# Two half-array matmuls for the second pass of the grouped-query scores

## The reference

```python
def attend(q, k, v):
    ...
    def block(qi):
        s = jnp.einsum('bkgqd,bksd->bkgqs', qi, k).astype(F32) * scale
        p = jax.nn.softmax(s, axis=-1).astype(v.dtype)
        return jnp.einsum('bkgqs,bkse->bkgqe', p, v)
...
gq_x = axial_rope(rms_norm(heads(x_gq, GQA_HEADS), gqa_q_norm_w[i]), ang_gqa)
gk_x = axial_rope(rms_norm(heads(x_gk, GQA_KV_HEADS), gqa_k_norm_w[i]), ang_gqa)
o_gqa = attend(gq_x, jnp.concatenate([gk_c, gk_x], axis=2), jnp.concatenate([gv_c, gv_x], axis=2))
```

## Time and profile before

| | |
|---|---|
| median of 3 runs | 3417.54 us (3416.53 to 3421.4) |
| the profiled execution | 3418.68 us |
| its span, first to last instruction | 3416.9 us |
| PE busy | 3356.0 us (98%) |
| DVE busy | 2267.3 us (66%) |
| ACT busy | 1252.6 us (37%) |
| POOL busy | 1012.0 us (30%) |
| mean granted TensorE clock | 0.997 |

### The profile page before, as it was taken

One profiled execution on the slowest core, in us unless ns is written; L12 is line 12 of the kernel. 1 busy time (PEld: TensorE's weight loads), 2 busy tenths in 40 slices (PEclk: granted clock), 3 DMA queues, 4 the chain that ended last, 5 costly groups with the idle time before them and its releaser, 6 DMA issues. The chain is left out here.

```text
span 3416.9 us, 49584 instructions
## 1 busy us (share of the span) xinstructions
PE 3356.0 (98%) x18300; PEld 2858.2 (84%) x18300; DVE 2267.3 (66%) x3536; ACT 1252.6 (37%) x2128; POOL 1012.0 (30%) x1121
## 2 busy tenths in 40 slices
PE   8999999999999999999999999999999999999998
PEld 4888888888888888888888788889998788888886
DVE  6574667887178888888855533478993656656566
ACT  4332356776142111111112532366773322222222
POOL 0232320111423333333334211410013343443433
PEclk9999999999999999999999999999999999999999
DMA  6455463121112222222110423562212111111111
GB/s 241 147 187 186 146 190 93 53 70 70 39 56 74 74 74 74 74 74 74 55 37 31 160 100 137 162 201 55 58 53 82 44 49 43 55 43 49 49 43 62
DMA packets 96241, 304.30 MB, mean 89 GB/s; under 512 B 11872, under 2 KB 38624, under 8 KB 93920
## 3 DMA queue, kind: packets, MB, share of 16 engines
q1 hardware_dynamic: 96096, 302.34, 27.0%
HBM read 239.12 MB, written 63.18 MB: 88 GB/s over the span
## 5 line engine op out<-in xcount | busy, mean ns | idle before, releaser
L131 POOL TENSOR_TENSOR wlo<-raw,whi 128x256 fp32r<-128x256 f32 x516 | 510.3, 1019 | 902.4 <-ACT whi L119 902.4
L2288 DVE SCALAR_TENSOR_TENSOR xT<-down_acc,mod,xT 128x512 f32<-128x512 f32 (+1 forms) x800 | 496.4, 694 | 211.6 <-PE down_acc L194 209.4
L2009 POOL TENSOR_TENSOR hid_lo<-y,hid_hi 128x256 fp32r<-128x256 f32 (+1 forms) x189 | 161.2, 884 | 622.8 <-ACT hid_hi L2185 622.8
L2174 ACT ACTIVATE up<-up_acc 128x512 f32<-128x512 f32 (+1 forms) x210 | 115.5, 551 | 601.4 <-PE up_acc L194 601.2
L192 PE MATMUL up_acc<-mix_hi,whi 128*128 128x512 f32 (+1 forms) x875 | 324.9, 371 | 1.8 <-DVE mix_lo L503 0.9
L193 PE MATMUL up_acc<-mix_lo,whi 128*128 128x512 f32 (+1 forms) x875 | 322.3, 368 | 0.0
L194 PE MATMUL up_acc<-mix_hi,wlo 128*128 128x512 f32 (+1 forms) x875 | 321.8, 368 | 0.0
L192 PE MATMUL up_acc<-late_hi,whi 128*128 128x512 f32 (+1 forms) x860 | 316.5, 368 | 0.0
L193 PE MATMUL up_acc<-late_lo,whi 128*128 128x512 f32 (+1 forms) x860 | 316.3, 368 | 0.0
L194 PE MATMUL up_acc<-late_hi,wlo 128*128 128x512 f32 (+1 forms) x860 | 316.3, 368 | 0.0
L192 PE MATMUL down_acc<-hid_hi,first_whi 128*128 128x512 f32 (+1 forms) x825 | 304.5, 369 | 1.4 <-DVE xT L2334 1.4
(11 more groups left out here) (334 smaller groups left out, 7604.2 us busy)
## 6 DMA issues: line engine op xcount, KB each, us to landing
raw<-in_w_rest SPq DMA_DIRECT2D x112, 512.0 KB, 3.7
norm_buf<-in_w_ada SPq DMA_DIRECT2D x52, 768.0 KB, 4.4
first_raw<-in_w_rest SPq DMA_DIRECT2D x57, 512.0 KB, 3.6
proj_scratch<-stage SPq DMA_DIRECT2D x18, 640.0 KB, 5.0
raw<-in_w_first SPq DMA_DIRECT2D x21, 512.0 KB, 6.2
ada_raw<-in_w_ada SPq DMA_DIRECT2D x6, 1536.0 KB, 14.1
xT<-proj_scratch SPq DMA_DIRECT2D x4, 1920.0 KB, 9.1
xT<-in_xT SPq DMA_DIRECT2D x8, 640.0 KB, 24.9
```

The costliest lines, as they stand in the source:

```text
L131: m = nc.gpsimd.tensor_tensor(self.lo[k][:, x:x + 256], self.raw[k][:, x:x + 256], self.hi[k][:, x:x + 256].bitcast(f32), ALU.subtract)
L2009: m = nc.gpsimd.tensor_tensor(hid_lo[:, x:z], y[1][:, x:z], hid_hi[:, x:z].bitcast(f32), ALU.subtract)
L2174: nc.scalar.activation(up[half][:, pc:pc + w], ub[c][:, :w], ACT.Copy).then_inc(up_evac, 1)
L2288: nc.vector.scalar_tensor_tensor(xs, db[g % DB][:, :w], mod_of(layer, 5, m, c), xs, ALU.mult, ALU.add).then_inc(added, 1)
```

## The change

The second pass of the first two pieces of a latent GQA block needs only the high keys, so each of its matmuls uses 64 of the 128 rows: the first piece in rows 0 to 63, the second in rows 64 to 127. As `ks[i]` holds the high keys in one half only, the 512 keys that are wanted in the other half are kept a second time, in `kx` (512 columns of the new tile `key_again`). The order becomes: wait for piece 0, pass 1 of piece 0, wait for piece 1, pass 1 of piece 1, pass 2 of piece 0 in 64 rows (this one raises `s_first`), pass 2 of piece 1 in 64 rows, then piece 2 as before. The products of low queries and low keys drop out in these two pieces. There are two more loads in each layer, and `ks_in` is awaited at 96. `key_again` takes 8 KB of each partition, and the scratch area for dynamic transfers is set to 8192 bytes.

```diff
@@ -195,6 +195,7 @@
+    key_again = ms.sb("key_again", [P, 2048], f32r)
     xT = ms.sb("xT", [P, KB, TOK])
@@ -1053,6 +1054,7 @@
             ks = [s.sb(f"ks{i}", [P, TOK], f32r) for i in range(GKV)]
+            kx = key_again[:, 120:632]
@@ -1137,6 +1139,8 @@
                 for i in range(GKV):
                     for part in range(2):
                         sp.dma_start(ks[i][(part ^ i) * HD:(part ^ i) * HD + HD, :].bitcast(f32), gk_d[part, i * HD:(i + 1) * HD, :]).then_inc(ks_in, 16)
+                    other = slice((1 - i) * HD, (2 - i) * HD)
+                    sp.dma_start(kx[other, :].bitcast(f32), gk_d[0, i * HD:(i + 1) * HD, (1 - i) * 512:(2 - i) * 512]).then_inc(ks_in, 16)
@@ -1194,7 +1198,7 @@
                         if h == MH:
-                            pe.wait_ge(ks_in, 64)
+                            pe.wait_ge(ks_in, 96)
@@ -1206,6 +1210,17 @@
                         c0, w = k0 * P, (k1 - k0) * P
+                        if not is_mla(h) and not is_ctx(n) and p < 2:
+                            q, k = terms(h)[0]
+                            nc.tensor.matmul(S[n % 2][:, c0:c0 + w], q[:, b * P:(b + 1) * P], k[:, c0:c0 + w], start=True, stop=False)
+                            if p == 1:
+                                for half in range(2):
+                                    rows, c0 = slice(half * HD, (half + 1) * HD), half * 512
+                                    k = ks[h % 2][rows, c0:c0 + 512] if half == h % 2 else kx[rows, :]
+                                    mm = nc.tensor.matmul(S[n % 2][:, c0:c0 + 512], ql[h % 2][rows, b * P:(b + 1) * P], k, start=False, stop=True)
+                                    if half == 0:
+                                        mm.then_inc(s_first, 1)
+                            continue
                         for x, (q, k) in enumerate(terms(h)):
@@ -2524,7 +2539,7 @@
-    nc = bacc.Bacc("TRN2", target_bir_lowering=False, num_devices=1)
+    nc = bacc.Bacc("TRN2", target_bir_lowering=False, num_devices=1, dynamic_dma_scratch_size=8192)
```

## The result

| | before | after |
|---|---|---|
| median | 3418.07 us (3416.53 to 3421.4, 4 runs) | 3458.74 us (3456.74 to 3458.85, 4 runs) |
| profiled execution | 3418.68 us | 3456.74 us |
| its span | 3416.9 us | 3454.9 us |

The ratio is 1.0116, 95% interval 1.0099 to 1.0134: slower by 40.7 us, where the forecast said 25 (3443.5) and the range ended at 3466. Executions of one kernel differ by up to 5.7 us in the runs of this document.

The account below looks back on a forecast made before the run. TensorE looked like the bound, DVE close behind in grouped-query attention. Layer 1 +12.7, layer 0 +12.1, entries +2.8, ends -2.8 gave +24.8 on 3418.7: 3443.5 us; own range 3436 to 3450, extended into rival 1 to 3466.

Parts of the forecast that it names:

- the loop: Grouped-query blocks: low parts, PE's pass 1 of piece 1, first half-matmul, maximum, next low parts; 4.04 us against 3.775.
- The saving: Scores, second pass of two pieces: PE issues one 512-column matmul less, 0.24 us in 96 blocks, at most 23 us.
- the half-matmul's part of the loop: From PE's released matmul to DVE's first maximum: 0.34 to the half-matmul, 0.40 its length, 0.03 to DVE's start.
- Rival 1: Scores: PE drains between full-array and half-array work; loop grows 0.16 to 0.27 us, 3459 to 3469 us; chance 0.23.
- entries: Start of each layer 0 head: first_part of blocks 0 and 1 comes 0.24 us later, +2.8 us in all.
- ends: End of a head before context blocks, and of the stage: some -0.4 us, seven times, -2.8 us.
- What ends later still: Check of PE and ACT per block: PE waits even after output transposes, 5.35 against release at 5.37; neither reaches 4.04.
- One link: DVE, from the start of first_part to the next low parts: two maxima in written order, 1.94 us of the loop.
- Rival 2: Grouped-query stages: PE's saved matmul is won, needing first_part by 1.83 us after the low parts; -23, 3396 us; chance 0.07.
- Rival 3: Grouped-query stages: no change, DVE's existing waits absorb most of the signal's delay; 3412 to 3424 us; chance 0.05.
- Rival 4: Scores: the halves run one after the other, PE issues as much as before; 3446 us at most; chance within forecast's 0.65.
- Costed at nothing: Four new loads, the wait for 96, new tile and smaller scratch: taken to cost no time.

Follow-up runs that it names:

- experiment 1: Kernel before with the new order of scores matmuls, all of them in the full array: 3441.16 us, ratio 1.0065.
- experiment 2: Kernel before in its old order, but first_part of grouped-query blocks waits for the block's last matmul: 3461.0 us, ratio 1.0123.
- experiments 3 and 4: First maximum of grouped-query blocks reads a long-loaded buffer without waiting, exponent takes a constant: changed kernel 3440.62 us, kernel before 3415.55 us.
- experiment 7: Changed kernel with both half-matmuls in the same 64 rows, the copied keys loaded but unused: 3468.76 us, ratio 1.0144.
- experiment 5: Kernel before in its old order, only pass 2 of the first piece made one 64-row matmul in its old place: 3453.53 us, ratio 1.0103.
- experiment 8: Changed kernel with the scores matmuls of the kernel before; new tile, loads, smaller scratch and wait for 96 stay: 3418.69 us, ratio 0.9999.
- experiment 10: Kernel before in its old order, all six scores matmuls of a latent grouped-query block in 64 rows: 3440.21 us, ratio 1.0061.
- experiment 6: Changed kernel with halves for second and third piece instead, first piece with two full passes raising s_first early: 3436.89 us, ratio 1.0057.
- 9: Kernel before in its old order, pass 2 of first and second piece each one 64-row matmul in its old place: 3487.37 us, ratio 1.02.

## Why the prediction was right, point by point

- *What bounds the stage, and the loop.* Right, and shown: experiment 1 has the loop without a single half-matmul, experiment 2 lengthens it and pays as computed, experiments 3 and 4 open it. My 4.04 us a block gave 3443.5; with the order alone it is 4.00 in layer 1 and 3441.2. In layer 1 PE waits for L1393 at a pass 1 in 43 of the 48 blocks, 13.7 us in all.
- *The saving.* It exists as a stretch of PE (experiment 7: 0.23 us a block) and is lost twice over: by the loop, and by the mode changes around it, 0.38 us, which exceed it. I had PE doing less than before. Its own work in the scores grew instead from 1.24 to 1.41 us (2503.13 to 2504.54) after a fold.
- *The term that was mis-sized* is the half-matmul's part of the loop: 0.34 + 0.40 + 0.03 = 0.77 forecast, 0.43 + 0.50 + 0.04 = 0.97 measured. Rival 1 had priced that at +0.16 to +0.27, and it is +0.20: the forecast and this rival were both true, one as the mechanism, the other as its size, and I had held them apart with 0.65 and 0.23. The forecast's own range ended at 3450, and the measured 3458.7 lies outside it, at the low edge of rival 1's 3459 to 3469; it is in the stated range only because that went on into rival 1. Even the rival's size came in part by luck. It let half 0 start 0.50 after the release, with up to 0.11 more for its load, and gave the half-matmul itself nothing more; measured are 0.43, 0.07 before the end that the trace gives to pass 1 (2507.57 + 0.50), and a half-matmul longer by 0.10. The full sum: loops in layer 1, 48 x (4.185 - 4.04) = +7.0 over the forecast; in layer 0 the six intervals of a head take 24.9 and 25.1 (25.45 in the first) for the forecast 24.2, +5; entries 0.73 a head for 0.48, +1.5; ends -0.13 each for -0.4, +2. That is 24.8 + 15.5 = 40.3, against 40.2 in the two stages and 40.7 between the medians.
- *What ends later still.* I wrote that PE always waits, by a hair after a fold with output transposes. With 0.39 us more from the low parts to the transposes it doesn't (2497.74 to 2500.27, 2.53 for the forecast 2.14): in those blocks PE comes to the scores only at L + 1.33 (2503.13 against 2501.80), piece 1 is already free, and the step is 4.44 us instead of 4.24.
- *One link was shorter.* From the first maximum to the next low parts I took 1.94. In blocks without `normalise` it is 1.76 (2508.54 to 2510.30), so the blocks alternate between 4.24 and 4.06. The 1.93 that I read for such a block before held a wait for the block's last matmul: its second maximum started 0.74 after the first (2487.51 to 2488.25), and 0.60 now (2508.54 to 2509.14). So the pace in layer 1 is 4.04, plus 0.20 for the half-matmul, less 0.09 on average for this link, plus 0.03 for the few blocks of 4.44: 4.18, measured 4.185. With the half-matmul alone mis-sized it would have been 4.24.
- *Rival 1, the drain.* The trace agrees with it in part. From pass 1 to the halves after a stall it has 0.43 us, where a stall within the full array has 0.34. Weight loads stood 0.25 us for nothing the profile shows (2508.43); those of the halves did so in all 96 blocks, 26.0 us in all. Each change has its price: 0.09 in, 0.19 out, 0.09 at the next matmul (experiment 5). The last part stands behind a matmul whose load starts with it and not under the matmul before (2508.43; 2497.53 in experiment 5): in experiment 5 the next one comes 0.33 us later, as in the earlier trace rows after the stall (0.34). A full drain is not shown, as half 0 starts 0.07 before pass 1 has ended by the trace. The 0.07 us behind the fold that I held for the rival says nothing of rows: the trace gives the fold and the scores behind it both as 128*128.
- *Rival 2 (faster)* needed the first maximum by L + 1.83; it came at L + 2.30. *Rival 3 (no change)* fell with it. *Rival 4* did not happen: the halves overlap (both start at 2508.00).
- *Costed at nothing:* the tile, the loads, the scratch and the wait for 96, right (experiment 8: 0.9999). That a weight load runs under the matmul before it holds within the full array: in experiment 5 full matmuls start 0.23 apart with a load of 0.19 each. At a change of mode it does not: the halves' loads start with the halves (2508.00) and none runs under pass 1, and the halves came 0.43 after pass 1 where I had 0.34.
- *Small slips:* the first head of layer 0 took 22.65 us before and not 22.43 (0.2 us of the sum), and the lower end of the forecast's own range comes to 3437 by its terms, not 3436. Neither decides anything. No run shows the 0.05 us by which that lower end lets a half-matmul end sooner: measured are 0.49 to 0.50 us right after a full one and 0.39 after another half (experiment 10), where a full one in a stream has 0.39 to 0.40.

The two causes do not add. The order alone is +22, the new form on PE with the loop open +25, both +41. A block takes the longer of the loop and PE's own work, so the longer hides a part of the other; besides, PE's wait for piece 1 is in both figures. How the 6 us between the sum and the whole divide was not measured. No version here beats the kernel before. The nearest, with nothing to wait for at the first maximum, is 0.9991 and is not the same computation, so at most 3 to 4 us lie in that wait.

## What to carry to other kernels

When a change reorders matmuls to save one, ask first which semaphore now fires behind which wait, and add up the loop through it: a loop's length is the floor of the pace, and it can rise while no engine has more to do (experiment 1: 4.00 us a block for 3.775). Here two half-array matmuls at once saved one stream time and paid for entering and leaving the mode. At 0.24 us saved (0.12 in experiment 6) and 0.32 to 0.38 us paid, one pair a block lost even with `s_first` left early (+17.9 us, experiment 6). By these numbers two pairs of 512 columns in one stay would save 0.48 and so begin to win on PE; that is an estimate, and no run here has more than one pair. If two cases in a forecast can both be true, price them together.

## What the hardware showed that I had not expected

- A round trip between full-array and 64-row matmuls of the scores costs PE 0.38 us in its stream and 0.36 us of time a block (34.5 us over 96 blocks, 68.8 for two, experiments 5 and 9). Where it ends in the transposes it costs less: 0.32 us of stream in experiment 6, 0.22 us of time in experiment 10.
- A half-matmul of 512 columns right after a full one lasts 0.49 to 0.50 us, one after another half 0.39. The first full one after a half lasts 0.50 as well (2497.53).
- Two half-matmuls in different rows start within 0.01 us of each other; in the same rows the second costs 0.23 us more (experiment 7).
